# Alternating two kinds of attention steps in a fused two-block transformer kernel

## The chip, the cores and the metric

The kernel runs on one core of a Trainium2 chip. The metric is device time in microseconds (us) for one execution, lower is better. The profile is one execution taken by the hardware profiler; its times count from the first instruction.

## What is computed

Two transformer blocks in float32 on one sequence of 512 positions, width 1024. Only the second mixer of the first block bears on this change:

```python
def odd_mixer(h, ...):
    # eight stick-breaking heads of 64 (o_c), eight latent heads (o_d)
    ...
    q_full = heads(rmsnorm(c_q, q_norm) @ w_uq, H_MLA, NOPE_DIM + ROPE_DIM)
    q_nope, q_rope = q_full[..., :NOPE_DIM], rope(q_full[..., NOPE_DIM:], positions)
    kv_full = heads(rmsnorm(c_kv, kv_norm) @ w_ukv, H_MLA, NOPE_DIM + V_DIM)
    ...
    o = jnp.concatenate([o_c.reshape(b, s, W_SB), o_d.reshape(b, s, W_MLA)], axis=-1)
    return o @ w_out
```

Stick-breaking attention weighs key j for query i with exp(z_ij - sum over k from j to i of softplus(z_ik)). The latent attention is a softmax over chunks of 64, with queries and keys of 96 (64 projected and 32 rotated, the rotated keys shared by all heads).

## The kernel before

Everything is transposed: features in the partitions, the 512 positions in the free dimension. Each weight is streamed once as a slab of 128 x 1024 float32 (8 tiles of 128 x 128). SyncE loads slab m into `raw[m % 2]`; ScalarE copies its two halves to `w_hi` (L1051), rounded; GpSimd subtracts to get `w_lo` (L455). Slab m + 2 is split when the product of slab m is full (`slab_done`, L1053). A product of a tile is three matmuls, high x high, high x low, low x high (L480 to L482; L635 to L637 in `early_out`). Three PSUM banks `gemm_banks` take the projections in a ring that is worked out ahead (`ring`, L115). VectorE evacuates them.

The mixer has 8 pairs of heads, p = 0 to 3 stick-breaking and p = 4 to 7 latent, and four blocks of 128 queries each: 32 steps, `s = 4 p + i`, block i with keys 0 to w = 128 (i + 1). A step's scores for both heads go to two of the four `score_banks` (bank pair b = s % 2). Each engine runs its own program in order; semaphores join them. In iteration s of the loop, TensorE (L811) does: scores of step s (L758, L765), projection tiles (`cd_beside(s, 0)`), transposes of the shares of step s - 1 back into its score banks (`cd_flip`, L773), more tiles, for stick-breaking the mask of step s + 1 as a matmul (`cd_bias`, L746), and the values of step s - 1 into `out_bank` (`cd_values`, L787).

A stick-breaking step: ScalarE computes Abs (L1295), Exp (L1296), Relu (L1302) and Ln (L1303) of the scores of both heads at a time; VectorE scans them from right to left for each head (L1890) and subtracts (L1892); ScalarE takes Exp (L1300). A latent step: VectorE adds the mask and takes row maxima (L1693), ScalarE exponentiates with row sums (L1144), VectorE takes reciprocals (L1904), ScalarE scales (L1152). For both, VectorE copies the turned shares from PSUM (`cd_take`, L1899) before `cd_values` can use them. When the four blocks of a pair are done, ScalarE copies `out_bank` to `u_hi` (L1307) and VectorE subtracts to get `u_lo` (L1908); the next pair's first values wait for that.

`CD_ITEMS` (L182) lists the projections in order: v, q, k of each stick-breaking pair with 8 tiles each, then, for each latent pair, c0, c1 (keys and values of its heads, 2 tiles each) and q0, q1 (3 tiles each), packed without gaps into 5 slabs. Values are transposed on TensorE in between (`vt`). 30 tiles come before step 0; `cd_plan` (L187) gives the rest, by halves of a step: six or seven a step in steps 0 to 10, two or three from step 11 to 26. From step 27 on, `EARLY` (L642) puts tiles of the first two columns of the output projection beside the steps; they need the finished `u_hi`, `u_lo` of a pair.

Of the kernel before, what the change touches and what calls it, by code (L numbers as in the profile page):

```python
# [39 lines left out]
P = 128  # L40
# [134 lines left out]
def half(s, side):  # L175
# [6 lines left out]
CD_ITEMS = [(name, p, 8) for p in range(4) for name in "vqk"] + \  # L182
           [(name, p, n) for p in range(4, 8) for name, n in (("c0", 2), ("c1", 2), ("q0", 3), ("q1", 3))]
STICK_STEPS, CD_STEPS, CD_AHEAD = 16, 32, 30


def cd_plan():  # L187


    at, out = CD_AHEAD, {}  # L190
    for s in range(27):
        if s < 11:
            sides = (4, 2) if s == 0 else ((3, 2), (4, 2), (4, 2), (4, 3))[s % 4]
        else:
            sides = ((1, 2), (1, 1), (1, 1), (1, 2))[(s - 11) % 4]
        for side in range(2):
            out[s, side] = (at, at + sides[side])
            at += sides[side]
    return out
# [9 lines left out]
def cd_evened(s):  # L209

    return 64 + (s + 1 if s < STICK_STEPS else 2 * (s + 1) - STICK_STEPS)
# [74 lines left out]
def build(nc, slabs, x_in, params_in, consts_in, pos1_in, pos2_in, rel_in, lam_in, y_out):  # L286
    n_slabs = slabs.shape[0]
    rel_rows = nc.dram_tensor("rel_rows", (8, E_LEN), F32, kind="Internal").ap()
    with ExitStack() as stack:
# [20 lines left out]
        q_t, k_t = sb("q_t", [2, S], F32, region), sb("k_t", [2, S], F32, region)  # L310
        region.close()
# [6 lines left out]
        V, VT = sb("V", [2, NB, P]), sb("VT", [S])  # L318
# [4 lines left out]
        wf = sb("wf", [KT, 40], F32R)  # L323
# [83 lines left out]
        slab_used = sem("slab_used")  # L407
# [7 lines left out]
        norm_full, mean_ready, gate_ready = sem("norm_full"), sem("mean_ready"), sem("gate_ready")  # L415

# [49 lines left out]
        def _(pe):  # L466
# [156 lines left out]
            def early_out(n, low, high):  # L623
# [4 lines left out]
                for kt in range(low, high):  # L628
                    if kt % 4 == 0:
                        pe.wait_ge(slab_split, c.slab.at(2 * n + 1 + kt // 4, 2))  # L630
                    pe.wait_ge(act_lo, c.lo.at(kt + 1))
# [3 lines left out]
                    pe.matmul(bank, high_w, u_hi[:, kt, :], start=kt == 0, stop=False, skip_group_check=True)  # L635
                    pe.matmul(bank, high_w, u_lo[:, kt, :], start=False, stop=False, skip_group_check=True)
                    last = pe.matmul(bank, low_w, u_hi[:, kt, :], start=False, stop=kt == KT - 1,  # L637
# [67 lines left out]
            marks["cd_lo"] = cd_lo  # L705

            def cd_products(low, high):
                for name, p, j, n in units(CD_ITEMS, low, high):
                    at = cd_banks[name, p]
                    if name == "vt":  # L710
                        pe.wait_ge(gemm_free, done["v" if p < 4 else "c1", p])
                        bank = open_ring(at)
                        for t in range(NB):
                            last = pe.transpose(bank[:, t * P:(t + 1) * P], VT[:, t * P:(t + 1) * P], ident)
                    else:
# [20 lines left out]
                        if j < n - 1:  # L736
                            continue
# [1635 lines left out]
```

## Time and profile before

| | us |
|---|---|
| median of 3 runs (2112.16 to 2114.46) | 2112.99 |
| the profiled execution | 2108.83 |
| its span, first to last instruction | 2107.0 |
| TensorE busy in the span | 2032.5 |
| steps of the mixer that the change touches, from 681 to 880.5 | 199.5 |

TensorE's busy time counts modelled ends of pipelined matmuls, so a start-to-start distance (0.23 us for a 512-column matmul) is shorter than a matmul's shown 0.39 us, and the end of each busy stretch hides a little of the wait behind it. Idle of an engine is put down to what released it last.

### The profile page before, as it was taken

The numbers are of one execution on the slowest core, as the hardware profiler recorded it, in microseconds if no ns is written. First come the engines' busy times: TensorE is split into PE (matmuls) and PEld (weight loads), VectorE is DVE, ScalarE is ACT, GpSimd is POOL, SyncE is SP. The second block draws the span as 40 slices with busy tenths as digits, with TensorE's granted clock in tenths as the row PEclk, the third lists the DMA queues.
The fourth block names the chain that finished last, engine by engine and source line by source line (L and its number), as shares of the span: only waits on it lengthen the run. The fifth ranks groups of instructions, "written<-read, shape, count | busy, mean of one in ns | idle before, by whom it ended". The sixth has DMA issues, their size and how long they took to land.

```text
span 2107.0 us, 28472 instructions
## 1 busy us (share of the span) xinstructions
PE 2032.5 (96%) x9900; PEld 1601.9 (76%) x9900; DVE 972.4 (46%) x1563; ACT 902.2 (43%) x1759; POOL 870.6 (41%) x648
## 2 busy tenths in 40 slices
PE   9999999999999988899999999999999999999997
PEld 6777688888887755688888886766667888888886
DVE  7444545322354678542312265557565653323133
ACT  5444443323344664442323346656554333223234
POOL 3222345444454321254444453542113554445454
PEclk9999999999999999999999999999999999999999
DMA  4222122222222110122322222221111323223323
GB/s 146 71 71 84 57 100 93 97 100 93 97 100 90 61 41 31 41 93 97 100 94 96 100 92 78 90 93 49 40 41 61 100 90 100 100 90 100 100 90 110
DMA packets 50581, 177.88 MB, mean 84 GB/s; under 512 B 5536, under 2 KB 5800, under 8 KB 50480
## 3 DMA queue, kind: packets, MB, share of 16 engines
q1 hardware_dynamic: 48096, 172.07, 24.6%
q10 hardware_dynamic: 2384, 4.43, 0.6%
q8 instruction: 67, 1.10, 0.2%
q14 instruction: 34, 0.28, 0.0%
HBM read 174.36 MB, written 2.12 MB: 84 GB/s over the span
## 4 chain that ended last, share of the span: by engine, by line
issue 47%; PE 30%; POOL 19%; DVE 2%; POOLq 1%; ACT 0%; DVEq 0%; ACTq 0%
POOL w_lo L455 19%; PE gemm_banks L480 9%; PE gemm_banks L481 9%; PE gemm_banks L482 9%; PE score_banks L934 1%; PE out_bank L980 1%; PE score_banks L943 1%; DVE turned L2117 1%; POOLq L449 0%; POOLq L454 0%; PE gemm_banks L906 0%; DVE score_banks L1693 0%; DVE x L2213 0%; PE out_bank L971 0%; ACT tmp L1395 0%
## 5 line engine op out<-in xcount | busy, mean ns | idle before, releaser
L455 POOL TENSOR_TENSOR w_lo<-raw,w_hi 128x512 fp32r<-128x512 f32 x644 | 870.4, 1374 | 1219.2 <-ACT w_hi L1051 1219.1
L1051 ACT ACTIVATE w_hi<-raw 128x512 fp32r<-128x512 f32 x644 | 371.0, 624 | 825.1 <-PE gemm_banks L482 810.0
L480 PE MATMUL gemm_banks<-h_hi,w_hi 128*128 128x512 f32 x1512 | 611.8, 405 | 3.4 <-POOL w_lo L455 3.1
L482 PE MATMUL gemm_banks<-h_hi,w_lo 128*128 128x512 f32 x1512 | 590.5, 391 | 0.0
L481 PE MATMUL gemm_banks<-h_lo,w_hi 128*128 128x512 f32 x1512 | 590.0, 390 | 0.0
L480 PEld LDWEIGHTS gemm_banks<-h_hi,w_hi 128*128 128x128 f32 x1512 | 283.2, 187 | 93.6 <-issue 32.0
L480 PE MATMUL gemm_banks<-u_hi,w_hi 128*128 128x512 f32 x848 | 330.3, 390 | 4.2 <-POOL w_lo L455 2.9
L482 PEld LDWEIGHTS gemm_banks<-h_hi,w_lo 128*128 128x128 f32 x1512 | 282.9, 187 | 62.1
L482 PE MATMUL gemm_banks<-u_hi,w_lo 128*128 128x512 f32 x848 | 329.9, 389 | 0.0
L481 PE MATMUL gemm_banks<-u_lo,w_hi 128*128 128x512 f32 x848 | 329.9, 389 | 0.0
L481 PEld LDWEIGHTS gemm_banks<-h_lo,w_hi 128*128 128x128 f32 x1512 | 283.7, 188 | 56.4 <-issue 2.6
L1601 DVE TENSOR_TENSOR x<-gemm_banks,x 128x512 f32<-128x512 f32 x112 | 77.5, 692 | 308.0 <-PE gemm_banks L482 305.8
L480 PEld LDWEIGHTS gemm_banks<-u_hi,w_hi 128*128 128x128 f32 x848 | 159.1, 188 | 38.9 <-issue 3.7
L482 PEld LDWEIGHTS gemm_banks<-u_hi,w_lo 128*128 128x128 f32 x848 | 159.2, 188 | 33.0
L481 PEld LDWEIGHTS gemm_banks<-u_lo,w_hi 128*128 128x128 f32 x848 | 159.2, 188 | 33.0
L1801 DVE TENSOR_TENSOR u_lo<-tmp,u_hi 128x512 fp32r<-128x512 f32 x86 | 108.6, 1263 | 125.6 <-ACT u_hi L1237 108.7
L1144 ACT ACTIVATE probs<-score_banks,top 128x128 f32<-128x128 f32 (+3 forms) x192 | 99.4, 523 | 140.4 <-DVE top L1693 137.4
L1152 ACT ACTIVATE probs<-probs,share 128x128 f32<-128x128 f32 (+3 forms) x160 | 81.1, 554 | 73.2 <-DVE share L1715 36.1
L1537 DVE TENSOR_TENSOR tmp<-gemm_banks,rstd 128x512 f32<-128x512 f32 x52 | 36.0, 692 | 141.0 <-PE gemm_banks L482 139.6
L1793 DVE SCALAR_TENSOR_TENSOR tmp<-gemm_banks,rstd 128x512 f32<-128x512 f32 x64 | 44.3, 692 | 121.2 <-PE gemm_banks L482 118.5
L1556 DVE TENSOR_TENSOR acc<-acc,sq 128x512 f32<-128x512 f32 x51 | 71.0, 1392 | 10.1 <-ACT sq L1069 9.3
L1693 DVE CUSTOM_DVE_ANT_0 score_banks<-score_banks,sin 128x128 f32<-128x128 f32 (+3 forms) x96 | 45.4, 514 | 35.7 <-PE score_banks L934 35.5
(314 smaller groups left out, 1884.6 us busy)
## 6 DMA issues: line engine op xcount, KB each, us to landing
raw<-slabs SPq DMA_DIRECT2D x322, 512.0 KB, 3.3
table<-rel_rows ACTq DMA_DIRECT2D x4, 512.0 KB, 3.4
x<-x_t SPq DMA_DIRECT2D x4, 256.0 KB, 6.9
x<-x_t ACTq DMA_DIRECT2D x4, 256.0 KB, 7.1
cos<-pos SPq DMA_DIRECT2D x2, 256.0 KB, 10.3
y_t<-x SPq DMA_DIRECT2D x2, 256.0 KB, 2.8
y_t<-x ACTq DMA_DIRECT2D x2, 256.0 KB, 2.7
y_t<-x SPq DMA_DIRECT2D x1, 512.0 KB, 2.8
```

The lines of the kernel that those rows point to most:

```text
L455: pool.tensor_tensor(w_lo[:, j, part], raw[:, j, part], w_hi[:, j, part].bitcast(F32), ALU.subtract).then_inc(slab_split, 1)
L480: pe.matmul(out, high, rhs_hi, start=first, stop=False)
L481: pe.matmul(out, high, rhs_lo, start=False, stop=False)
L482: return pe.matmul(out, low, rhs_hi, start=False, stop=last)
L1051: act.activation(w_hi[:, m % 2, part], raw[:, m % 2, part], ACT.Copy).then_inc(slab_hi, 1)
L1144: act.activation(probs[:, b, head, 0:w], SC[:, 2 * b + head, 0:w], ACT.Exp, bias=top[:, b, head:head + 1], scale=-1.0, accum_out=mass[:, b ...
L1152: act.activation(probs[:, b, head, 0:w], probs[:, b, head, 0:w], ACT.Copy, scale=share[:, b, head:head + 1]).then_inc(evened, 1)
L1556: dve.tensor_tensor(sums[:, :], sums[:, :], sq[:, c.acc.slot, :], ALU.add).then_inc(acc_ready, 1)
L1601: dve.tensor_tensor(x[:, j, :], bank, x[:, j, :], ALU.add).then_inc(gemm_free, 1)
L1693: last = dve.tensor_tensor_reduce(z, z, masks[head], -1.0, 3e38, ALU.add, ALU.min, top[:, b, head:head + 1])
L1793: dve.scalar_tensor_tensor(tmp[:, s, :], result(), 0.0, rstd[:, :], ALU.max, ALU.mult).then_inc(gemm_free, 1)
L1801: dve.tensor_tensor(u_lo[:, j, :], tmp[:, 2 + s, :], u_hi[:, j, :].bitcast(F32), ALU.subtract).then_inc(act_lo, 1)
```

## The change

The 32 steps get a new order: stick-breaking step n, then latent step n - 2. So the order is S0, S1, S2, L0, S3, L1, and so on to S15, L13, L14, L15. Score banks still go by s % 2. The projections are reordered to suit: the latent weights of pair p + 3 are taken before those of stick-breaking pair p. Each latent pair has two slabs of its own (c with 4 tiles, q with 6 tiles), so the stage takes 15 slabs for stick-breaking and latent pairs where it took 12 and 5: three more in all.

- The plan spreads the tiles over steps 0 to 23; the early output tiles, taken in the order in which pairs finish (0, 4, 1, 5, 2, 6, 3, 7), go beside steps 24 to 32.
- The output is handed over by block: after each step ScalarE copies 128 columns of `out_bank` (`cd_mixed(s - 2)`, the first thing in iteration s), VectorE subtracts, and the values of step s wait for that of step s - 1.
- The stick-breaking chain goes by heads: Ln, scan, subtraction and last Exp are issued for one head and then the other, and the transposes of head 0 wait for head 0's shares only. That last Exp is now at the head of the following iteration on ScalarE.
- In a latent iteration that follows a stick-breaking one, VectorE does maxima, output block, take of the stick-breaking shares and reciprocals, and only then evacuates the results of three halves.
- Buffers: stick-breaking q and k in `tmp`, latent values in `V_late`, `VT_late`, `wf` in a region used later; the shared rotated keys are copied in steps 0 and 1.

The core of the diff:

```diff
+for p in range(1, 4):
+    CD_ITEMS += latent("c0", "c1", p=p + 3) + [("v", p, KT)] + latent("q0", "q1", p=p + 3) + [("q", p, KT), ("k", p, KT)]
+CD_ITEMS += latent("c0", "c1", "q0", "q1", p=7)
+CD_ORDER = [(k // NB + 4 * odd, k % NB) for n in range(18) for k, odd in ((n, 0), (n - 2, 1)) if 0 <= k < 16]
+CD_AT = {step: t for t, step in enumerate(CD_ORDER)}
+CD_STEPS, CD_AHEAD = len(CD_ORDER), 31
...
+    twin = ((2, 2), (2, 1), (2, 2), (2, 2), (3, 2), (2, 2), (3, 2), (3, 2))
+    sides = ((4, 2), (4, 2), (2, 2), (2, 2), (3, 2), (2, 2)) + twin + twin + ((2, 2), (2, 2))
...
             def cd_flip(s):
-                pe.wait_ge(evened, cd_evened(s))
                 for head in range(2):
+                    pe.wait_ge(evened, 64 + 2 * s + head + 1)
...
             def cd_values(s):
                 pe.wait_ge(taken, AB_STEPS + s + 1)
                 if i == 0:
                     pe.wait_ge(gemm_free, done["vt", p])
-                    if p >= 1:
-                        pe.wait_ge(act_lo, cd_lo + C_TILES + p)
+                if s >= 1:
+                    pe.wait_ge(block_out, s)
...
+            CD_EARLY = {(24, 0): (0, 0, 1), (24, 1): (0, 1, 2), (25, 0): (0, 2, 3), (25, 1): (0, 3, 4),
+                        (26, 0): (0, 4, 5), (26, 1): (1, 0, 1), (27, 0): (1, 1, 2), (27, 1): (1, 2, 3),
+                        (28, 0): (1, 3, 4), (28, 1): (1, 4, 5), (29, 1): (0, 5, 6), (30, 0): (1, 5, 6),
+                        (31, 1): (0, 6, 7), (32, 0): (1, 6, 7)}
...
+            def stick_shares(s):
+                kind, p, i, b, w = cd_step(s)
+                for head in range(2):
+                    if head == 0:
+                        act.wait_ge(lessened, cd_count("stick", s))
+                    else:
+                        act.wait_ge(maxed, AB_STEPS + s + 1)
+                    act.activation(probs[:, b, head, 0:w], probs[:, b, head, 0:w], ACT.Exp).then_inc(evened, 1)
...
+                for head in range(2):
+                    act.activation(part[:, head, :], part[:, head, :], ACT.Ln, bias=ones[:, 0:1]).then_inc(softened, 1)
...
+            for s in range(CD_STEPS + 2):
+                kind = cd_kind(s)
+                if s >= 2:
+                    cd_mixed(s - 2)
+                if kind == "stick":
+                    soften(s)
+                elif kind == "latent":
+                    if cd_kind(s - 1) == "stick":
+                        stick_shares(s - 1)
+                    weigh(AB_STEPS + s, cd_step(s)[4])
                 cd_products(*cd_half(s, 0))
+                if kind == "latent":
+                    even(s, cd_step(s)[4], AB_STEPS + cd_count("latent", s))
                 cd_products(*cd_half(s, 1))
...
+                    dve.wait_ge(softened, 2 * cd_count("stick", s) + head - 1)
                     back = soft[:, b, head, 0:w][:, ::-1]
+                    link(dve.tensor_tensor_scan(back, back, positive[:, head, 0:w][:, ::-1], 0.0, ALU.add, ALU.add))
+                    last = dve.tensor_tensor(probs[:, b, head, 0:w], z[:, head, :], soft[:, b, head, 0:w], ALU.subtract)
+                    last.then_inc(maxed if head else lessened, 1)
...
+            for s in range(CD_STEPS + 2):
+                kind = cd_kind(s)
+                twin = kind == "latent" and cd_kind(s - 1) == "stick"
+                if kind == "latent":
+                    w = cd_step(s)[4]
+                    maxima(AB_STEPS + s, w, [chunk_mask[:, S - w:S]] * 2)
+                if s >= 2:
+                    cd_mixed(s - 2)
+                if twin:
+                    cd_take(s - 1)
+                    cd_shares(s)
+                    cd_evacuated(*cd_half(s - 1, 1))
+                cd_evacuated(*cd_half(s, 0))
+                if not twin and 1 <= s <= CD_STEPS:
+                    cd_take(s - 1)
+                if kind == "stick":
+                    stick(s)
+                elif kind == "latent" and not twin:
+                    cd_shares(s)
+                if cd_kind(s) != "stick" or cd_kind(s + 1) != "latent":
+                    cd_evacuated(*cd_half(s, 1))
```

## Rows read from the trace of the kernel before

**Rows 1.** The page, part 1: busy us of the engines, share of the span.

```profile
PE 2032.5 (96%) x9900; PEld 1601.9 (76%) x9900; DVE 972.4 (46%) x1563; ACT 902.2 (43%) x1759; POOL 870.6 (41%) x648
```

**Rows 2.** Busy us by window: length, PE, PEld, DVE, ACT, POOL, PEclk, DMA share, GB/s.

```profile
681.00:755.80 74.80, 73.67 (x422) 54.09 (x420) 48.35 (x56) 47.32 (x74) 23.11 (x17) 1.00 0.19 64
755.80:850.00 94.20, 75.20 (x451) 52.07 (x449) 76.97 (x146) 49.23 (x105) 12.56 (x10) 0.96 0.09 29
850.00:880.50 30.50, 26.05 (x167) 17.91 (x165) 15.16 (x37) 13.73 (x35) 2.96 (x2) 1.00 0.06 18
...
780.00:790.00 10.00, 7.78 (x43) 5.42 (x43) 9.63 (x11) 5.72 (x7) 3.44 (x2) 0.83 0.15 52
```

**Rows 3.** Waits from 681 to 882 us: who waited for whom, total us, times, longest.

```profile
POOL w_lo L455 <- ACT w_hi L1051: 161.7, 15, 27.5
...
PE out_bank L787 <- DVE turned L1899: 11.8, 14, 2.4
PE score_banks L773 <- ACT probs L1300: 10.7, 7, 2.2
```

**Rows 4.** Timeline of PE, a dense stretch: start us, us, engine, line, operation.

```profile
726.12 0.66 PE L787 MATMUL out_bank<-turned,V 128*64 128x128 f32 x8
726.71 1.13 PE L765 MATMUL score_banks<-k_t,q_t 64*128 64x512 f32 x4
727.77 0.50 PE L480 MATMUL gemm_banks<-h_hi,w_hi 128*128 128x512 f32 x1
...
728.57 0.40 PE L480 MATMUL gemm_banks<-h_hi,w_hi 128*128 128x512 f32 x1
...
729.26 0.39 PE L480 MATMUL gemm_banks<-h_hi,w_hi 128*128 128x512 f32 x1
```

**Rows 5.** Timeline of PE, a thin stretch (idle before and releaser in brackets).

```profile
785.77 1.54 PE L773 MATMUL score_banks<-consts,probs 128*128 128x128 f32 x6 [2.22 <-ACT probs L1300]
786.96 0.78 PE L480 MATMUL gemm_banks<-cn_hi,w_hi 128*128 128x512 f32 x1
...
793.13 1.09 PE L773 MATMUL score_banks<-consts,probs 128*128 128x128 f32 x8 [1.41 <-ACT probs L1300]
793.98 0.48 PE L480 MATMUL gemm_banks<-cn_hi,w_hi 128*128 128x512 f32 x1
```

**Rows 6.** Groups of VectorE by form, 680 to 882 us: busy us, mean ns.

```profile
L1899 DVE COPY turned<-score_banks 128x1024 f32<-128x1024 f32 x8 | 9.8, 1225 | 8.6 <-PE score_banks L773 5.0 <-issue 3.6
L1890 DVE TENSOR_TENSOR_SCAN soft<-soft,c_raw 128x512 f32<-128x512 f32 x8 | 9.4, 1212 | 0.1
...
L1876 DVE SCALAR_TENSOR_TENSOR tmp<-gemm_banks,sin 32x512 f32<-32x512 f32 x8 | 5.6, 695 | 0.1
...
L1693 DVE CUSTOM_DVE_ANT_0 score_banks<-score_banks,c_raw 128x512 f32<-128x512 f32 x8 | 5.5, 702 | 2.0 <-PE score_banks L758 1.9
L1899 DVE COPY turned<-score_banks 128x512 f32<-128x512 f32 x8 | 5.5, 690 | 5.7 <-PE score_banks L773 5.7
...
L1899 DVE COPY turned<-score_banks 128x256 f32<-128x256 f32 x8 | 3.3, 417 | 1.6 <-PE score_banks L773 1.5
```

**Rows 7.** Groups of ScalarE by form, the same stretch.

```profile
L1303 ACT ACTIVATE soft<-soft,consts 128x1024 f32<-128x1024 f32 x4 | 4.6, 1142 | 0.0
...
L1296 ACT ACTIVATE soft<-soft 128x1024 f32<-128x1024 f32 x4 | 4.2, 1060 | 0.1
...
L1295 ACT ACTIVATE soft<-score_banks 128x1024 f32<-128x1024 f32 x4 | 4.1, 1028 | 4.0 <-PE score_banks L765 4.0
L1302 ACT ACTIVATE c_raw<-score_banks 128x1024 f32<-128x1024 f32 x4 | 4.0, 1005 | 0.0
```

**Rows 8.** Timelines of GpSimd (POOL) and VectorE: two 128-column scans, twice.

```profile
710.92 2.64 POOL L455 TENSOR_TENSOR w_lo<-raw,w_hi 128x512 fp32r<-128x512 f32 x2 [9.31 <-ACT w_hi L1051]
...
712.04 1.80 DVE L1890 TENSOR_TENSOR_SCAN soft<-soft,c_raw 128x128 f32<-128x128 f32 x2
...
769.18 0.73 DVE L1890 TENSOR_TENSOR_SCAN soft<-soft,c_raw 128x128 f32<-128x128 f32 x2
```

More of the change, by code:

```diff
@@ L206, in cd_half, with cd_step, cd_kind, cd_count @@
     return CD_PLAN.get((s, side), (0, 0))
-def cd_evened(s):
-    return 64 + (s + 1 if s < STICK_STEPS else 2 * (s + 1) - STICK_STEPS)
+def cd_step(s):
+    p, i = CD_ORDER[s]
+    return "stick" if p < 4 else "latent", p, i, s % 2, (i + 1) * P
+def cd_kind(s):
+    return cd_step(s)[0] if 0 <= s < CD_STEPS else None
+def cd_count(kind, s):
+    return sum(cd_kind(n) == kind for n in range(s + 1))
 E_BASE, DIFF_STEPS, E_STEPS, E_AHEAD = 64, 16, 48, 6
@@ L627, in early_out @@
                     pe.wait_ge(gemm_free, c.gemm.at(n - 1))
[L628 to L631, printed above, removed]
+                for k in range(low, high):
+                    kt = k
+                    if mixed is not None:
+                        kt = mixed[k]
+                        if k == 0:
+                            pe.wait_ge(slab_split, c.slab.at(2 * n + 2, 2))
+                        pe.wait_ge(block_out, CD_AT[kt, NB - 1] + 1)
+                    else:
+                        if kt % 4 == 0:
+                            pe.wait_ge(slab_split, c.slab.at(2 * n + 1 + kt // 4, 2))
+                        pe.wait_ge(act_lo, c.lo.at(kt + 1))
                     w_slot = (c.slab.now + n) % 2
@@ L817, in _ @@
                 cd_beside(s, 1)
-                if s + 1 < STICK_STEPS:
+                if cd_kind(s + 1) == "stick":
                     cd_bias(s + 1)
@@ L1854, in cd_evacuated @@
                     c.gemm.now += 1
-                    if p >= 4 and name != "vt":
-                        dve.wait_ge(scored, 64 + 8 * (p - 1))
                     if name == "vt":
-                        if p >= 2:
-                            dve.wait_ge(valued, 64 + 8 * (p - 1))
-                        last = dve.tensor_copy(V[:, p % 2, :, :], bank)
+                        if p not in (0, 1, 4, 5):
+                            dve.wait_ge(valued, 64 + 2 * (CD_AT[p - 2, NB - 1] + 1))
+                        last = dve.tensor_copy(cd_values_of(p), bank)
                     elif name == "v":
@@ L2261, in pack_slabs @@
     out += column_tiles(cq) + [slab(np.concatenate([kr, kr[:, 16:], kr[:, :16]], 1))] + column_tiles(ckv)
-    out += heads(w, 0)
-    tiles = []
-    for p in range(4):
-        pair = []
-        for h in (2 * p, 2 * p + 1):
-            uq, ukv = a["w_uq"][0][:, 96 * h:96 * h + 96], a["w_ukv"][0][:, P * h:P * (h + 1)]
-            pair.append((tiles_of(ukv), tiles_of(np.concatenate([uq, uq[:, 80:96], uq[:, 64:80]], 1))))
-        tiles += [t for part in range(2) for head in pair for t in head[part].transpose(1, 0, 2)]
-    out += [np.ascontiguousarray(np.stack(tiles[k:k + 8], 1)).reshape(P, SLAB) for k in range(0, len(tiles), 8)]
+    plain = heads(w, 0)
+    late = {}
+    for p in range(4, 8):
+        for part, wide in enumerate((P, 96)):
+            pair = []
+            for h in (2 * p - 8, 2 * p - 7):
+                if part == 0:
+                    m = a["w_ukv"][0][:, P * h:P * (h + 1)]
+                else:
+                    m = a["w_uq"][0][:, wide * h:wide * (h + 1)]
+                    m = np.concatenate([m, m[:, 80:96], m[:, 64:80]], 1)
+                pair.append(m)
+            late["cq"[part], p] = slab(np.concatenate(pair, 0))
+    for name, p, n in CD_ITEMS:
+        if p < 4:
+            out.append(plain[3 * p + "vqk".index(name)])
+        elif name in ("c0", "q0"):
+            out.append(late[name[0], p])
     out += column_tiles(a["w_out_cd"][0]) + mlp(1)
```

209 lines of the change are left out of this document (77 added, 132 removed).

## The prediction

> **What bounds the kernel now.** The page first: TensorE (PE) has work for 96% of the span [rows 1], so time can only come from its gaps, and from work that moves into them. The windows of the stage that is changed show where they are [rows 2]. The stage runs from 681 to 880.5 us, 199.5 us. Its first 11 steps (681 to 755.8) are dense: PE idles 1.1 of 74.8 us. From 755.8 to 850 it idles 19.0 of 94.2 us, from 850 to 880.5 another 4.4 of 30.5. The waits name two causes, on PE [rows 3]: `cd_values` waits for the copy of the turned shares (VectorE, 11.8 us), `cd_flip` for the last Exp of a stick-breaking step (10.7 us). In the first 11 steps the same chain is hidden by projection tiles: a tile of three matmuls costs 0.69 us from start to start (728.57 to 729.26), 0.80 where it is the first after other work (727.77 to 728.57) [rows 4], and there are 66 of them beside 11 steps, six a step. From step 11 on two or three stand beside a step, while the latent steps come one after another. So the bound is latency for want of filler, not any engine's capacity: VectorE, the next busiest, is busy 48.4 + 77.0 + 15.2 = 140.5 of 199.5 us [rows 2]. The idle also lowers PE's clock: six turns after a wait of 2.22 us take 1.19 us (785.77 to 786.96), where eight took 0.85 at 793.13, and the granted clock from 780 to 790 is 0.83 of 2.4 GHz, that is, part of it at 1.2 GHz [rows 2, 5].
>
> **PE's own demand.** 66 tiles x 0.69 = 45.5 us of the first 74.8; less 1.1 idle, the other 28.2 us are eleven steps' scores, turns, values and first-tile surcharges, some 2.5 us a step. Before, the stage holds 106 projection tiles and 16 early output tiles: 122 x 0.69 = 84, and 32 x 2.5 = 80, together 164. The stage therefore loses 199.5 - 164 = 35.5 us: 24.6 seen as idle, the rest hidden under modelled matmul ends and in the slower clock. That is all that the change can win.
>
> **1. The order.** Each latent step now follows a stick-breaking step two ahead of it, so the tiles are spread evenly: 105 beside steps 0 to 23 (4.4 a step), then output tiles, two a step in steps 24 to 28 and one a step in 29 to 32. Demand is 105 x 0.69 + 24 x 2.5 = 132.5 us for steps 0 to 23, 11.0 us a pair of steps, and 31 us for the tail. No instruction of PE is added or removed but one tile that moves ahead of the stage, where PE is busy: no gain from it.
>
> VectorE is what must keep pace. To its 140.5 us come: outputs by blocks of 128 columns, 32 subtractions where 8 were; a PSUM pass takes 0.690 for 512 columns and 0.417 for 256 [rows 6], so 0.28 for 128: 32 x 0.28 - 8 x 0.69 = +3.5. The stick-breaking subtraction by heads costs one fixed part more, 2 x 0.417 - 0.690 = 0.14, x 16 = +2.3. Some 2 us of waits between scan and subtraction make it 148. The tail has no evacuations; at the durations of [rows 6] it holds nine takes (7.4), three steps' scans and subtractions (8.7), five steps' maxima (6.0) and small work (3): 25 us. That leaves 123 us for steps 0 to 23, 10.2 us a pair against PE's 11.0. Engines in order at 93% of each other do meet. Two places are visible in the plan: the turned values vt5 and vt6 (steps 9, 17) open a bank whose evacuation (v2, v3) is queued on VectorE behind the stick-breaking take and `cd_shares`, 1 to 2 us each; and around steps 9 to 10 and 17 to 18 two latent q results of 4 x 0.695 = 2.8 us each [rows 6] stand ahead of a take.
>
> What a pair loses is not in the trace. Bounds: nothing (the dense stretch loses 0.1 a step), or all in series, in the rival below. The rows between which it lies: 0.1 us a step at six tiles, 19.0/16 = 1.2 a step at 2.5 tiles; at 4.4 tiles that is 0.6 a step, 1.2 a pair. The chain is also shorter (2.), so I take 1.0: 12 us for twelve pairs.
>
> **2. The chain by heads.** Before, a 512-wide stick-breaking step needs from its scores to its turns Abs 1.03, Exp 1.06, Relu 1.00, Ln 1.14 [rows 7], with the step before's Exp among them, two scans of 1.21, a subtraction of 1.22 and an Exp of 1.06: 8.9 us and more. By heads the first head is ready after 1.03 + 1.06 + 1.00 + 0.57 + 1.21 + 0.69 + 0.53 = 6.1 us, the second after another scan and subtraction, 8.0 us. PE does the rest of step s and the first half of step s + 1 between these scores and their turns, 1.3 steps of 5.5, some 7 us in the middle of the stage: head 0 is covered and head 1 nearly. That the Exp is now behind the copy of the last output block costs nothing: that block's values end before the next scores, two PE items ahead of the turns.
>
> **3. The tail.** Steps 24 to 27 have two tiles each: I take 0.5 lost a step, 2 us. Step 28 is the last stick-breaking one, 512 wide, and PE has only two tiles, 1.6, small turns and values, 0.6, and the next scores, 0.8, before it needs the shares: 3.0 us. It waits about 8.0 - 3.0 - 0.4 = 4.6 us. The latent steps 29 to 32 have one tile where [rows 2] had two beside them and idled 4.4 us in six steps: 0.73 + 0.69 = 1.4 each, 5.7 us. The tail loses 12.3 in all.
>
> **4. Three more weight slabs** (latent weights no longer share slabs: 5 become 8), each with a 512 KB load, two ScalarE copies and two GpSimd subtractions. GpSimd waits 161.7 us for ScalarE in this stage [rows 3], and a slab of four latent tiles lasts PE about a step, 5 us, against the 2.6 us in which GpSimd splits one [rows 8]: taken at nothing; the upper bound is GpSimd's six operations in the open, 3 x 2.6 = 7.9 us, which stays inside the range. There is a side cost. Two scans of 128 columns take 0.73 us by themselves and 1.80 when they start beside the subtraction of w_lo [rows 8]. The Trainium skill, "SBUF — State Buffer" (Who interferes with whom), says that a VectorE instruction with two SBUF inputs blocks against a GpSimd one that reads SBUF; by it six more subtractions would give up to six more such blockings, an estimate of one subtraction's length each, and it speaks against the change. In the rows the delay is 1.80 - 0.73 = 1.07 us for a pair of scans, so at most 3.2 us of VectorE's time for three slabs. Scans (0.73 to 2.4 us a step, 16 steps) take 25 us, 13% of the stage, so most slabs meet none; what is left is inside the 1.0 a pair.
>
> **The sum.** Steps 0 to 23: 132.5 + 12 = 144.5; tail: 31 + 12.3 = 43.3; the stage 187.8 us against 199.5: 11.7 us less. The profiled execution took 2108.83 us with a span of 2107.0; it becomes 2097.1. The median of the runs is 4.2 us above it, and I put the same difference on that: 2113.0 - 11.7 = **2101.3 us**.
>
> **Rivals.** A: the pairs mesh, losing 0.2 a pair or less; only the tail costs. 132.5 + 2 + 43.3 = 178: 2091.5, or 2089 if half of step 28's wait is covered by head 0. For it: the first stretch loses next to nothing; against it: VectorE at 93%. B, little changes: a pair costs 12.7 to 13.4 us, because the late evacuations and blocked scans of 1. and 4. come in every pair and not in four. 2109 to 2117, about 2112. Against it: evacuations are 42 us (in steps 0 to 23 16 single ones, 6 results c of two operations and 8 results q of four, 60 x 0.695), a third of VectorE's work. C, slower: VectorE's queue puts everything into one loop in every pair: the take waits for the turns, with evacuations, maxima and the next stick-breaking step behind it. For 512 columns the loop is 8.0 + turns 0.85 + take 1.23 + values 1.2 (eight take 0.59) + scores 1.06 = 12.3 [rows 4 to 7]; over the four widths about 0.7 of it, 8.6; evacuations 42/12 = 3.5; maxima and output block 1.5: 13.6 a pair. 12 x 13.6 + 43.3 = 206.5, so 2120.0. It decides from 13.4 a pair on ((199.5 + 4.2 - 43.3)/12). Against it: maxima run while ScalarE and PE do the Exp and turns, and most evacuations while ScalarE softens.
>
> **Chances.** A measurement of this kernel can tell 0.2%, 4.2 us, from no change. The forecast, a pair between 11.2 and 12.7 us: 0.60; A 0.17; B 0.13; C 0.10. So faster 0.77, same 0.13, slower 0.10. Range 2089 to 2112: from A with a better tail to the middle of B.
>
> **What would show it.** Right: PE's waits in the stage fall from 24 to about 15 us; most sit after step 24, the longest, over 3 us, before the last stick-breaking turns; VectorE is busy about nine tenths of steps 0 to 23; the half clock shows only in the tail. The rest of the kernel keeps its length. Wrong: waits of over 1 us in each pair at `cd_flip` (chain) or at opening a bank (late evacuations), or PE waiting on w_lo in the stage (slabs).

## The result, and the profile after

The changed kernel took 2115.6 us (median of 20 runs), the kernel before 2112.9 (20 runs of its own): ratio 1.0015, 95% interval 1.0009 to 1.0022. The forecast was 2101.3 us and faster. The kernel became slower by about 3 us. That is less than the 4.2 us that the prediction needs to tell a time from no change, and it lies above the top of its range, 2112 us.

The profiled execution has a span of 2113.8 us, 6.8 more than before. 2.6 us of that is no part of the change: up to the norm matmul that opens this part of the mixer both kernels run the same instructions, and it stands at 670.12 us before, 672.75 after, and between 669.6 and 673.6 in the kernels below. All lengths here are therefore counted from that matmul to the first slab of the output projection that waits for its split weights ("norm to slab"): 670.12 to 882.15 = 212.0 us before, 672.75 to 888.58 = 215.8 after, 3.8 more. Of these, 2.6 lie ahead of the first mask matmul (10.89 us before, 13.46 after) and 1.2 in the steps. Behind the slab the two kernels are equal within 0.4 us.

The page, part 1, of the changed kernel (before: [rows 1]):

```profile
PE 2038.5 (96%) x9900; PEld 1604.6 (76%) x9900; DVE 974.3 (46%) x1603; ACT 914.3 (43%) x1821; POOL 877.6 (42%) x654
```

Windows of the changed kernel, columns as in [rows 2]: ahead of the steps, steps 0 to 23, a period of eight steps, the tail, and two stretches of the tail.

```profile
670.00:686.20 16.20, 14.94 (x64) 11.32 (x63) 14.06 (x20) 7.78 (x13) 6.29 (x5) 1.00 0.28 98
686.20:831.90 145.70, 134.69 (x792) 97.61 (x790) 109.91 (x209) 92.95 (x210) 42.16 (x32) 1.00 0.18 58
723.50:771.80 48.30, 45.07 (x271) 32.69 (x270) 36.05 (x71) 31.25 (x71) 13.72 (x11) 1.00 0.17 55
831.90:887.00 55.10, 40.85 (x242) 26.64 (x240) 31.09 (x65) 28.24 (x65) 2.94 (x2) 0.91 0.03 10
834.00:845.00 11.00, 8.29 (x38) 5.31 (x38) 8.77 (x18) 3.28 (x10) 1.33 (x1) 0.84 0.15 48
860.00:875.00 15.00, 9.98 (x52) 6.82 (x50) 7.84 (x17) 7.18 (x18) 0.00 (x0) 0.77 0.00 0
```

Steps 0 to 23 took 145.7 us where 144.5 was forecast: twelve pairs at 12.1, as the period of four pairs shows (48.3). The tail took 55.0 us (831.92 to 886.95) where 43.3 was forecast. And VectorE is busy 109.9 of 145.7 us, 75%, not nine tenths.

Waits of the changed kernel, 670 to 889 us (before: [rows 3]):

```profile
POOL w_lo L489 <- ACT w_hi L1088: 165.9, 20, 51.8
...
PE out_bank L823 <- DVE turned L1927: 9.1, 11, 1.7
...
PE score_banks L808 <- ACT probs L1317: 9.0, 9, 3.3
...
PE gemm_banks L754 <- DVE VT L1891: 2.7, 2, 1.3
...
PE gemm_banks L676 <- DVE c_raw L1889: 2.4, 1, 2.4
```

The two large groups fell by 2.7 and 1.7 us, and two new ones came: openings of a projection bank. The sum did not fall. PE's waits from the timeline are 11.0 us in steps 0 to 23 and 14.2 in the tail. Timeline of PE, one wait of steps 0 to 23 and those that open the tail and step 28's turns:

```profile
745.17 0.63 PE L754 MATMUL gemm_banks<-consts,c_raw 128*128 128x128 f32 x4 [1.33 <-DVE VT L1891]
...
831.92 0.70 PE L800 MATMUL score_banks<-tmp 64*128 64x256 f32 x4
834.98 0.50 PE L676 MATMUL gemm_banks<-u_hi,w_hi 128*128 128x512 f32 x1 [2.36 <-DVE c_raw L1889]
...
839.02 0.88 PE L823 MATMUL out_bank<-turned,V_late 128*64 128x128 f32 x12 [1.73 <-DVE turned L1927]
...
843.00 0.63 PE L677 MATMUL gemm_banks<-u_lo,w_hi 128*128 128x512 f32 x1
...
849.31 0.40 PE L678 MATMUL gemm_banks<-u_hi,w_lo 128*128 128x512 f32 x1
850.33 1.09 PE L823 MATMUL out_bank<-turned,V_late 128*64 128x128 f32 x16 [0.62 <-DVE turned L1927]
...
864.45 1.02 PE L808 MATMUL score_banks<-consts,probs 128*128 128x128 f32 x4 [3.31 <-ACT probs L1317]
866.31 1.12 PE L808 MATMUL score_banks<-consts,probs 128*128 128x128 f32 x4 [0.83 <-ACT probs L1317]
```

VectorE over the first two waits of the tail:

```profile
830.67 0.69 DVE L1902 SCALAR_TENSOR_TENSOR QT<-gemm_banks,cos 32x512 f32<-32x512 f32 x1
...
832.80 1.40 DVE L1907 TENSOR_TENSOR QT<-QT,kr 32x512 f32<-32x512 f32 x1
834.24 0.69 DVE L1889 COPY c_raw<-gemm_banks 128x512 f32<-128x512 f32 x1
834.96 0.69 DVE L1902 SCALAR_TENSOR_TENSOR QM<-gemm_banks,cos 32x512 f32<-32x512 f32 x1
...
837.09 0.68 DVE L1907 TENSOR_TENSOR QM<-QM,kr 32x512 f32<-32x512 f32 x1
837.81 0.29 DVE L1937 TENSOR_TENSOR u_lo<-out_bank,u_hi 128x128 fp32r<-128x128 f32 x1
838.02 0.95 DVE L1927 COPY turned<-score_banks 128x768 f32<-128x768 f32 x1
```

From 830.67 to 837.8 VectorE works off the last three results of the projections, 9 operations, though no step needs the two queries before step 27. The take of step 23's turned shares stands behind them; its turns ended at 836.4. PE waits for a bank, then for the take, and then runs at the half clock (843.00 to 843.42 between two matmuls, where they take 0.23 at 2.4 GHz). Windows of 2 us show two such stretches in the tail, from 841 to 844 and from 865 to 871, and none in steps 0 to 23.

### The profile page after: what moved, and what is told of

Its sections match the earlier page's. It is cut to its first block, busy times and chain, and to the rows that moved or that the text cites. A ratio compares the mean times of both kernels' runs of the same rounds, so it can differ in the third digit from the quotient of the medians.

```text
span 2113.8 us, 28584 instructions
## 1 busy us (share of the span) xinstructions
PE 2038.5 (96%) x9900; PEld 1604.6 (76%) x9900; DVE 974.3 (46%) x1603; ACT 914.3 (43%) x1821; POOL 877.6 (42%) x654
## 4 chain that ended last, share of the span: by engine, by line
issue 46%; PE 31%; POOL 19%; DVE 2%; POOLq 1%; ACT 0%; DVEq 0%; ACTq 0%
POOL w_lo L489 19%; PE gemm_banks L514 9%; PE gemm_banks L516 9%; PE gemm_banks L515 9%; PE score_banks L971 1%; PE out_bank L1017 1%; PE score_banks L980 1%; DVE turned L2146 1%; POOLq L483 0%; POOLq L488 0%; PE gemm_banks L943 0%; DVE score_banks L1723 0%; DVE x L2242 0%; PE out_bank L1008 0%; ACT tmp L1425 0%
```

## The experiments

The theory after this reading: the steps are as forecast, and the tail loses to (a) evacuations ahead of the take and (b) two tiles a step where step 28 leaves PE 3.3 us with nothing. Its rival: VectorE's load bounds the pairs, and the tail only shows it. Each kernel is timed against the kernel before; "norm to slab" is of its one profiled execution, in which 2 us can be the clock alone (last section).

| kernel | median, us | ratio (95%) | norm to slab |
|---|---|---|---|
| before | 2111.0 to 2112.9 | 1 | 212.0 |
| changed | 2115.6 | 1.0015 (1.0009 to 1.0022) | 215.8 |
| e1_tail | 2109.5 | 0.9992 (0.9983 to 1.0000) | 211.8 |
| e2_pre | 2115.3 | 1.0016 (1.0006 to 1.0025) | 216.2 |
| e3_joint | 2122.7 | 1.0057 (1.0043 to 1.0070) | 223.5 |
| e4_heads | 2110.3 | 0.9999 (0.9990 to 1.0008) | 212.2 |
| e5_less | 2106.5 | 0.9976 (0.9967 to 0.9985) | 208.4 |
| e6_take_first | 2113.6 | 1.0008 (0.9999 to 1.0017) | 216.1 |
| e7_swap | 2117.6 | 1.0029 (1.0017 to 1.0041) | 221.6 |
| e8_bank | 2114.9 | 1.0013 (1.0003 to 1.0024) | 215.9 |
| e9_last | 2108.8 | 0.9986 (0.9977 to 0.9995) | 211.7 |
| e10_value | 2107.2 | 0.9979 (0.9969 to 0.9989) | 208.3 |
| e11_less7 | 2110.0 | 0.9990 (0.9981 to 1.0000) | 212.3 |

**e1_tail**: the last projections over four steps, output tiles later.

```diff
-    sides = ((4, 2), (4, 2), (2, 2), (2, 2), (3, 2), (2, 2)) + twin + twin + ((2, 2), (2, 2))
+    sides = ((4, 2), (4, 2), (2, 2), (2, 2), (3, 2), (2, 2)) + twin + twin + ((1, 1), (1, 1), (1, 1), (1, 1))
...
+            CD_EARLY = {(26, 0): (0, 0, 1), (26, 1): (0, 1, 2), (27, 0): (0, 2, 3), (27, 1): (0, 3, 4),
+                        (28, 0): (0, 4, 6), (28, 1): (1, 0, 2), (29, 0): (1, 2, 4), (29, 1): (1, 4, 5),
+                        (30, 0): (1, 5, 6), (31, 1): (0, 6, 7), (32, 0): (1, 6, 7)}
```

> The changed kernel with other filler at the end: the last eight projection tiles go one to a half over steps 22 to 25, and the output tiles start at step 26, with six of them between the scores of step 28 and its turns. Theory T (the tail): in the changed kernel steps 0 to 23 take what was forecast (145.7 us), and the gain is lost after step 24, where the last evacuations stand in front of a take (PE waits of 2.36 and 1.73 us), where the last stick-breaking step waits 4.1 us, and where PE twice runs at half clock. Then this kernel is about 7 us faster than the changed one: 2108 to 2109, ratio 0.998 to kernel before; the wait before the turns of step 28 falls from 4.1 to about 1.5 us and the one of 2.36 us goes. Rival V (VectorE's time as such is the bound): the waits move to other steps, the ratio stays at 1.0015.

4.1 us less than the changed kernel in norm to slab, and 0.0023 less in the ratio, some 5 us, where 7 were expected. Its PE timeline: the first wait did not go but moved on to the take, and step 28's fell from 3.31 + 0.83 to 0.55 + 1.20. In all, PE's waits in the tail fell from 14.2 to 11.0 us, and the time at the half clock from 10 to 7.

```profile
832.98 0.88 PE L823 MATMUL out_bank<-turned,V_late 128*64 128x128 f32 x12 [2.84 <-DVE turned L1926]
...
859.55 0.66 PE L808 MATMUL score_banks<-consts,probs 128*128 128x128 f32 x4 [0.55 <-ACT probs L1316]
861.40 0.70 PE L808 MATMUL score_banks<-consts,probs 128*128 128x128 f32 x4 [1.20 <-ACT probs L1316]
```

**e2_pre**: v of pair 1 goes ahead of the first latent c tiles, so that these, and their waits, leave the stretch ahead of step 0.

```diff
-    CD_ITEMS += latent("c0", "c1", p=p + 3) + [("v", p, KT)] + latent("q0", "q1", p=p + 3) + [("q", p, KT), ("k", p, KT)]
+    CD_ITEMS += ([("v", p, KT)] if p == 1 else []) + latent("c0", "c1", p=p + 3) + ([("v", p, KT)] if p > 1 else [])
+    CD_ITEMS += latent("q0", "q1", p=p + 3) + [("q", p, KT), ("k", p, KT)]
```

> The changed kernel with the v result of stick-breaking pair 1 ahead of the first latent c results, so that no latent tile stands before step 0. Theory P: in the changed kernel the distance from the second norm matmul to the first mask matmul grew from 10.9 to 13.5 us, 0.7 for the tile moved and 1.3 of waits (0.38 and 0.88 us) at latent tiles whose inputs or bank are late; here it is 12.1 to 12.3 and the kernel 1.3 us faster than the changed one, ratio 1.0009. Rival: VectorE has the same work in steps 0 and 1 and the wait comes back there (beyond the 0.77 us at the first stick-breaking q tile): ratio 1.0015.

The norm to first mask fell from 13.46 to 11.58 us, and the steps grew from 202.4 to 204.6. The ratio stayed, 1.0016, as the rival said. Up to step 4 its PE timeline has, among others, waits of 0.24 and 0.47 us, which are new, and of 1.27 and 1.73 us, which were 0.77 and 1.28; and from 708 to 711 us PE ran at the half clock:

```profile
689.32 0.48 PE L515 MATMUL gemm_banks<-cn_hi,w_hi 128*128 128x512 f32 x1 [0.24 <-POOL w_lo L490]
693.82 0.63 PE L755 MATMUL gemm_banks<-consts,c_raw 128*128 128x128 f32 x4 [0.47 <-DVE c_raw L1900]
```

The work of the latent c results has to pass VectorE before step 3 either way; where it stands settles which matmul waits.

**e3_joint**: the changed kernel with Ln, scans, subtraction, Exp and turns for both heads together, as before. **e4_heads**: the kernel before with its chain by heads, nothing else.

```diff
-                    pe.wait_ge(evened, 64 + 2 * s + head + 1)
+                pe.wait_ge(evened, 64 + 2 * s + 2)
...
-                    last = dve.tensor_tensor(probs[:, b, head, 0:w], z[:, head, :], soft[:, b, head, 0:w], ALU.subtract)
+                dve.tensor_tensor(probs[:, b, :, 0:w], z, soft[:, b, :, 0:w], ALU.subtract).then_inc(maxed, 1)
```

> The changed kernel with one part undone: Ln, subtraction and last Exp of a stick-breaking step for both heads at a time, turns wait for both. Theory H (the split chain is worth its cost): a 512-wide step's shares are ready about 1.5 us later, and the steps of 384 and 512 columns (8 of 16) wait 0.7 to 1.5 us more at their turns: 6 us slower than the changed kernel, ratio 1.004. Rival F (the fixed parts of the extra instructions, 2.3 us on VectorE and as much on ScalarE, eat it): ratio 1.001 to 1.002.

> The kernel before with one part of the change alone: Ln, subtraction and last Exp of a stick-breaking step by heads, the turns of head 0 wait for head 0's shares only; order, plan and outputs as before. Theory H: of the 10.7 us that PE waits there for the last Exp, steps 11 to 15 give back about 1 us each: 5 us faster than before, ratio 0.9976. Rival F: more instructions on busy engines, nothing gained: 1.000.

PE's waits of e3_joint, and of e4_heads:

```profile
PE score_banks L808 <- ACT probs L1313: 18.1, 9, 5.9
PE out_bank L823 <- DVE turned L1922: 7.8, 11, 1.4
```

```profile
PE out_bank L787 <- DVE turned L1906: 11.7, 12, 3.3
PE score_banks L773 <- ACT probs L1304: 6.8, 6, 1.9
PE score_banks L746 <- DVE turned L1906: 2.3, 3, 1.7
```

The window of e4_heads to set beside the second of [rows 2]:

```profile
755.00:850.00 95.00, 78.54 (x446) 54.32 (x444) 76.25 (x149) 49.49 (x114) 13.99 (x10) 0.91 0.08 28
```

By heads is worth 7.6 us in the new order (223.5 against 215.8; 6.1 of them by step 24) and nothing in the old one. There the waits for shares fell from 10.7 [rows 3] to 6.8 us, single waits for the take rose to 3.3, and all of PE's waits in the stage fell by 3.1 us, from 23.9 to 20.8. The stage did not become shorter because PE ran at the half clock more: the granted clock was 0.91 in that window and 0.96 before, which is 8.6 against 3.8 us of full-speed time missing. The other executions bear it out: over all eleven of e4_heads the mean granted clock is 0.990, and over those of the kernel before beside them 0.992. That is again between 4 and 5 us of full-speed time. Why the clock fell although PE waited less is open.

**e5_less** leaves out the sine part of the latent queries' rotation and its addition (L1904, L1907) for all pairs; **e11_less7** leaves them out for the last pair alone.

```diff
-                        dve.scalar_tensor_tensor(kr[64:96, :], bank[96:128, :], MLA_SCALE, sin1[96:128, :], ALU.mult,
-                                                 ALU.mult)
-                        link(dve.tensor_scalar(dst[0:64, :], bank[0:64, :], MLA_SCALE, None, ALU.mult))
-                        last = dve.tensor_tensor(dst[64:96, :], dst[64:96, :], kr[64:96, :], ALU.add)
+                        last = dve.tensor_scalar(dst[0:64, :], bank[0:64, :], MLA_SCALE, None, ALU.mult)
```

> This kernel leaves out the sine part of the latent queries' rotation and the addition behind it: two of the four VectorE operations on each latent query result, some 16 x 0.69 = 11 us of VectorE's time in steps 0 to 23, and nothing of TensorE's. Theory (in steps 0 to 23 TensorE's own demand and the single waits at bank openings bound, the tail loses by what stands ahead of the take): steps 0 to 23 fall by 0 to 3 us only (a period of eight steps 47.5 to 48.3 us against 48.31), the tail by under 1.5 us; time 2111.5 to 2114.5 us. Rival (VectorE, nine tenths busy, bounds the pairs): its 11 us come back, steps 0 to 23 about 136 us, time about 2105 us.

> The changed kernel, which leaves out the sine part of the rotation and its addition for the last pair's two query results alone: four VectorE operations, 2.8 us, the last of them in iterations 23 and 24. Theory (the tail's first 8 us lose by evacuations that stand ahead of the take of step 23): step 24 to step 26 falls from 14.40 to about 9.6 us, as where this was left out in all pairs, more than the 2.8 us of the operations, since TensorE's half-speed stretch goes with the wait; all else is unchanged; 4.8 us less, about 2110.8 us, ratio 0.999 to 1.0. Rival (VectorE's load over the whole stage gave the gain): 0.25 of the 8 us, 2113.5 us, ratio 1.0005 to 1.0012.

e5_less is 0.0039, some 8 us, below the changed kernel in the ratio and 7.4 us in norm to slab, far more than the theory had expected and nearly what the rival had. But its timeline says where: 2.8 us ahead of step 4 (its scores at 36.51 us behind the norm matmul, not 39.29), 4.8 us between the scores of steps 24 and 26 (9.56, not 14.40), and nothing in a period: 48.31 us, as in the changed kernel, with four operations, 2.8 us, less for VectorE in it. So ahead of step 4 VectorE's load does count, 2.8 us for 2.8: there it is busy 33.1 of the 39.3 us from the norm matmul on, and PE's waits up to step 4 are 2.95 us. e11_less7 leaves that place alone: 9.56 us from step 24 to 26, and all before it as in the changed kernel. Its PE timeline:

```profile
829.67 0.50 PE L676 MATMUL gemm_banks<-u_hi,w_hi 128*128 128x512 f32 x1 [0.19 <-DVE c_raw L1889]
...
832.34 0.88 PE L823 MATMUL out_bank<-turned,V_late 128*64 128x128 f32 x12 [0.36 <-DVE turned L1930]
```

2.36 and 1.73 became 0.19 and 0.36 us, 3.5 less, and the half clock behind them went too. So four operations of 2.8 us (3.5 with the long one) cost 4.8. At the slab 3.5 of the 4.8 are left: half of the rest went where PE ran at the half clock once more, from 878 us on. The rival, a load over the whole stage, is out: a load that bounds could not be cut in the middle without effect. The theory of e5_less was wrong in a size: it gave the tail under 1.5 us.

**e8_bank**: the changed kernel, where the first output tile of the tail takes its bank without waiting for the last value tile's evacuation.

```diff
-                    pe.wait_ge(gemm_free, c.gemm.at(n - 1))
+                    pe.wait_ge(gemm_free, c.gemm.at(n - 1 if mixed is None or n else -2))
```

> The changed kernel, where the first output tile of the tail takes its bank without waiting for the last value tile's evacuation (2.36 us). Theory: what stands behind is late anyway, since the take of step 23 stands behind three evacuations: the wait moves on to the values, stage length unchanged within 0.7 us, 2115 to 2115.6 us. Rival (the opened bank alone costs the 2.36 us): 2113.2 us, ratio 1.0003.

```profile
833.26 0.50 PE L676 MATMUL gemm_banks<-u_hi,w_hi 128*128 128x512 f32 x1 [1.63 <-DVE QT L1907]
838.02 0.88 PE L823 MATMUL out_bank<-turned,V_late 128*64 128x128 f32 x12 [2.46 <-DVE turned L1927]
```

2.36 + 1.73 became 1.63 + 2.46: the same 4.09 us. To open the bank 0.7 us earlier gains nothing; the take's place in VectorE's queue sets the time.

**e6_take_first** (on e1_tail) and **e7_swap** (on the changed kernel): VectorE takes ahead of the projection half in every iteration without a latent step behind a stick-breaking one.

```diff
-                cd_evacuated(*cd_half(s, 0))
                 if not twin and 1 <= s <= CD_STEPS:
                     cd_take(s - 1)
+                cd_evacuated(*cd_half(s, 0))
```

> The tail's filler as in the run with the spread sides, and in every iteration that has no latent step behind a stick-breaking one VectorE takes the turned shares before it evacuates the projection half. Theory (the take waits in VectorE's queue behind evacuations that nothing needs yet): the wait of 2.84 us ahead of values(23) and the waits of 0.5 us in the middle go, 3 us less than with the spread sides alone: about 2106.5 us, ratio to the kernel before 0.9975 to 0.9985, norm matmul to end of stage 208.5 to 209.5 us against 211.77. Rival (the flips' end sets the take, and its order in the queue changes nothing, or the evacuation that is now later holds the next bank and the wait moves there): 2109.5 us, as with the spread sides.

> The changed kernel with the order of VectorE's take and projection half alone swapped in the iterations without a latent step behind a stick-breaking one. Theory: the 0.5 us waits in the middle go (some three to five of them), the tail's 2.36 and 1.73 us stay, since these evacuations belong to an iteration with a latent step: 1 to 2 us less than the changed kernel, 2113.5 to 2114.5 us, ratio 1.0007 to 1.0012. Rival (order of no account): 2115.5 us, ratio 1.0015.

Both were slower than what they started from, by 4.3 and 5.8 us in norm to slab (0.0016 and 0.0014 in the ratio, 3.4 and 3.0 us; the profiled execution of e7_swap is 2.8 us above its median). By step 24 it was 4.4 and 5.4: neither theory had that. VectorE, and then PE, of e6_take_first:

```profile
748.64 0.29 DVE L1936 TENSOR_TENSOR u_lo<-out_bank,u_hi 128x128 fp32r<-128x128 f32 x1
751.32 1.23 DVE L1926 COPY turned<-score_banks 128x1024 f32<-128x1024 f32 x1 [2.39 <-PE score_banks L808]
752.57 0.69 DVE L1901 SCALAR_TENSOR_TENSOR QM<-gemm_banks,cos 32x512 f32<-32x512 f32 x1
```

```profile
698.18 0.50 PE L514 MATMUL gemm_banks<-h_hi,w_hi 128*128 128x512 f32 x1 [2.65 <-DVE QT L1906]
...
755.48 0.46 PE L793 MATMUL score_banks<-KT,QT 96*128 96x128 f32 x2 [1.79 <-issue]
```

A take that stands first waits for the turns, 2.39 us in which VectorE could have evacuated; the next latent scores need that query and come 1.8 us late. The expectation had counted the 0.5 us waits that would go and not what would then wait. The waits are the smaller part, though: in steps 0 to 23 they sum to 12.4 us against 10.7 in e1_tail, and to 11.3 against 11.0 in e7_swap. The larger part goes with the half clock, which came behind some of the long waits (from 700 and 806 us in e6_take_first; from 699, 757 and 808 in e7_swap) and which neither e1_tail nor the changed kernel has before the tail: the granted clock of steps 0 to 23 is 0.98 and 0.95 against 1.00. Only where the query is not needed soon is the swap a gain: from step 24 to 26 e6 took 11.8 us, e1_tail 13.6. The next two use this.

**e9_last**: e1_tail, and the take first in iteration 24 alone. **e10_value**: e9_last, and in iterations 9 and 17 the value tile is evacuated ahead of the reciprocals.

```diff
-                    cd_shares(s)
-                    cd_evacuated(*cd_half(s - 1, 1))
+                    if s in (9, 17):
+                        cd_evacuated(*cd_half(s - 1, 1))
+                        cd_shares(s)
+                    else:
+                        cd_shares(s)
+                        cd_evacuated(*cd_half(s - 1, 1))
+                if s == 24:
+                    cd_take(s - 1)
                 cd_evacuated(*cd_half(s, 0))
-                if not twin and 1 <= s <= CD_STEPS:
+                if not twin and 1 <= s <= CD_STEPS and s != 24:
```

> The kernel with the spread sides, where VectorE takes the turned shares ahead of the projection half in iteration 24 alone (there the half is the last rotated query, four operations). Theory (each such swap is worth what the tile's evacuation held up, less what then waits for the evacuation; in iteration 24 nothing needs that query before iteration 27): step 24 to step 26 takes 11.8 us as with the swap everywhere, against 13.57, and the stage's other parts stay as with the spread sides: norm matmul to the end of the stage 206.5 to 208 us (third tile behind the last values) against 209.44; time about 2107.7 us, ratio 0.998 to 0.9988. Rival: the swap brings nothing in sum, since the scores behind are late by as much: 2109.5 us, ratio 0.9992.

> As the run before, and in iterations 9 and 17 VectorE evacuates the value tile, for whose bank TensorE waits 1.33 us, ahead of the reciprocals, which there wait 0.40 us for ScalarE. Theory: each of the two waits falls by some 0.5 us, since the evacuation starts at the end of the take instead of behind wait and reciprocal; the eight-step period falls from 48.3 to 47.8 us, the time by 1 us to some 2106.7, ratio 0.9975 to 0.9985. Rival: the reciprocals come 0.3 to 0.5 us later, with them the scaled shares and their turns, and the period stays 48.3 us; 2107.7 us.

In e9_last step 24 to 26 fell to 11.9 us as expected, but norm to slab by 0.1 only: its tail has three stretches at the half clock (from 838, 862 and 879 us), that of e1_tail has two, and from step 28's scores to the slab it took 32.4 us against 31.0. e10_value, VectorE and PE in iteration 9:

```profile
740.05 0.69 DVE L1926 COPY turned<-score_banks 128x512 f32<-128x512 f32 x1 [0.29 <-PE score_banks L808]
740.65 0.68 DVE L1890 TENSOR_TENSOR VT<-gemm_banks,rstd 128x512 f32<-128x512 f32 x1
741.37 0.17 DVE L1931 RECIPROCAL share<-mass 128x2 f32<-128x2 f32 x1
```

```profile
741.48 0.63 PE L754 MATMUL gemm_banks<-consts,c_raw 128*128 128x128 f32 x4 [0.78 <-DVE VT L1890]
```

1.33 became 0.78 us, twice, and steps 0 to 23 fell by 1.2 us, a period from 48.3 to 47.7. The other 2.3 us that norm to slab is below e9_last are clock (last section). This version beats both kernels, if by 0.2% only: its interval of ratios, 0.9969 to 0.9989, lies below 1 and below that of the changed kernel. Against e9_last the intervals overlap. Its windows, steps 0 to 23 and tail:

```profile
683.04:824.50 141.46, 131.79 (x776) 94.84 (x774) 106.15 (x204) 91.62 (x207) 42.10 (x32) 1.00 0.17 57
824.50:876.40 51.90, 40.43 (x258) 26.54 (x256) 33.33 (x69) 29.73 (x68) 2.96 (x2) 1.00 0.06 20
```

## Why the prediction was wrong

From the norm matmul to the slab the forecast was 11.7 us less, and the profiled executions show 3.8 more. The 15.5 us between them are 2.6 ahead of step 0, 1.2 in steps 0 to 23 and 11.7 in the tail.

**Steps 0 to 23 were right**: 145.7 against 144.5 us, 11.0 us of visible waits against 12 lost. Most places were right too: openings for the turned values in iterations 9 and 17, 1.33 us each (forecast 1 to 2), and shares or takes late around 10 and 18 by 0.5 us. The reason given for them was half wrong: VectorE was to be nine tenths busy and is 75%. Its total of 141.0 us in steps and tail is that of before (140.5 [rows 2]) and not 148: blocks and heads did add, but the first c results (2.8 us) moved ahead of step 0, the scans took 2.4 us less, and 2 us of the 148 were waits. And the tail holds 31 us, not 25. From step 4 on, what costs is the order at a few places, not the load, as the unchanged period of e5_less shows. Not foreseen were the waits up to step 4, 2.95 us, where the same run shows VectorE's load to count.

**The term that failed is the tail**, "tail: 31 + 12.3 = 43.3" (31 of demand, 12.3 of loss), with 55.0 measured. Term by term:
- "I take 0.5 lost a step, 2 us" for steps 24 to 27: 6.0 us of waits (2.36, 1.73, 0.62, 0.91, 0.35). The prediction said "the tail has no evacuations". But the tiles of the last half of step 23 are evacuated in the tail, and two of the last three results are queries with four operations each. e11_less7 shows it: 4.8 us. The same queue had been priced for steps 9 and 17 and was forgotten here.
- The half clock was foreseen in the tail and priced at nothing. A granted clock of 0.84 over 11 us and of 0.77 over 15 us means 3.5 and 6.9 us at 1.2 GHz. Half of such time is lost, less what PE waits in it: some 4 us, an estimate. The first stretch's part of it is inside e11_less7's 4.8.
- Step 28: 4.6 us forecast, 3.31 + 0.83 = 4.1 measured. Steps 29 to 32: 5.7 forecast, 0.83 + 1.16 + 1.32 + 0.73 = 4.0 measured. Both right within their size.
- The demand, "31 us for the tail": 55.0 less 14.2 of waits and some 4 of clock leaves 37. e10_value, whose tail runs at 2.4 GHz throughout, agrees: 51.9 us from step 24's scores to the end of the steps, less 11.5 of waits and four more tiles (2.8), is 37.6. Not all of it is demand. A stop costs more than its shown wait: from 849.31 to 850.33 pass 1.02 us, of which a matmul takes 0.23 and the wait is given as 0.62, so 0.17 is hidden. Over the tail this sums to some 2.6 us, an estimate from the start-to-start distances of the same items where no wait follows. That leaves some 34.5, 3.5 more than forecast. Reasons visible in the rows, not tested: the turns and values of step 23 (0.58 and 0.81 us) fall into the tail, and the 2.5 us a step come from eleven stick-breaking steps of some 300 columns, while the tail's steps are 368 columns wide on average and five of the eight are latent. A latent step's scores of 512 columns take 1.83 us, in the rows below, and a stick-breaking one's 1.06 [rows 4].

```profile
875.13 1.12 PE L793 MATMUL score_banks<-KT,QT 96*128 96x512 f32 x2
876.10 1.02 PE L793 MATMUL score_banks<-KM,QM 96*128 96x512 f32 x2
876.96 0.82 PE L808 MATMUL score_banks<-consts,probs 128*128 128x128 f32 x6
```

Together: 4 (steps 24 to 27) + 4 (clock) - 2 (steps 28 to 32) + 2.6 (hidden) + 3.5 (demand) = 12 us, the 11.7 that are missing. The first term is shown by an experiment. The clock is read from the rows; the last two are estimates and, with the clock, not separated by one.

**"No gain from it", one tile that moves ahead**, was held at nothing and cost 2.6 us: the tile's 0.69, 0.38 of issue and 0.88 of waiting for VectorE, and the rest around these two stops. VectorE is busy 11.4 of the 13.5 us from the norm matmul to the first mask (8.7 of 10.9 before). e2_pre shows that it cannot be had back simply by moving the tiles.

**By heads** had no price of its own but stood behind the 1.0 a pair; e3_joint shows that this rests on it: a period of eight steps takes 50.4 us without it, 48.3 with it. **Three more slabs at nothing** was right: GpSimd still waits 165.9 us for ScalarE, PE's only wait for `w_lo` is the one behind the stage, 1.47 us as before, and the scans take 31.5 us in all against 33.9 before (the prediction had counted 25 for them). Ten of the 32 scans still met a slab's subtraction and took 0.3 to 0.7 us longer than their like, 5.4 us in all against 9.2 before. So did the rotated query's addition at 832.80, 1.40 us against 0.68 for the same at 837.09: 0.7 us in the worst place. GpSimd beside it:

```profile
832.39 2.94 POOL L489 TENSOR_TENSOR w_lo<-raw,w_hi 128x512 fp32r<-128x512 f32 x2 [5.20 <-ACT w_hi L1088]
```

The Trainium skill's page "SBUF — State Buffer" (Who interferes with whom) lists exactly this pair, a VectorE instruction with two SBUF inputs against a GpSimd one that reads SBUF, as contending; this row agrees.

The check named in the prediction, "PE's waits in the stage fall from 24 to about 15", failed: they sum to 25.2. So did "VectorE is busy about nine tenths". Held did that most waits sit after step 24, the longest, 3.31 us, before the last stick-breaking turns, and that the half clock shows only in the tail. That the rest of the kernel keeps its length held behind the stage (0.4 us) but not ahead of step 0 (2.6 us). Of the rivals none happened. The time lies in the 2109 to 2117 of B, but by chance: a pair costs 12.1 us, not the 12.7 to 13.4 that B needs.

So the gain was not hidden: the change does what it says in 24 steps, and gives it back in the eight that follow, where the filler is used up, plus 2.6 us ahead of the first. With the filler spread and VectorE's queue reordered in three iterations, the same change is 4 to 5 us faster than the kernel before. Some 3.5 of the forecast 11.7 us were never there, by the estimate above, since the demand of the tail was put too low.

## What to carry to other kernels

When filler is spread evenly over a loop, price the drain by its own instruction list, result by result, and not by the averages of the full stretch: the last results are evacuated after their tiles, in front of what the next step needs. Moving a copy forward in an in-order queue is a gain only where what falls behind it has slack; check for each place who needs that and when, and change only the places with slack. An engine at 75% can hold up the others at a few points: here, cutting its load in the eight-step periods gave nothing, and the same cut ahead of step 4 and in the drain gave 2.8 and 4.8 us. Compare the granted clock before a difference is put down to waits: in e4_heads, e6_take_first and e7_swap it moved by more than the waits did.

## What the runs showed of the hardware

The clock that TensorE is granted differs between executions of one kernel. Of the 20 of the changed kernel the two slowest (2118.7 and 2119.8 us) have the lowest mean clock, 0.987 and 0.986, and the four fastest (2112.2 to 2113.3 us) have 0.991 to 0.993.

Nor does it follow from the instructions and waits at hand alone. In e9_last and e10_value the tail from step 28 on is the same program with the same waits to 0.1 us, up to the slab's (0.88 and 1.47 us). e9_last had one stretch at the half clock before, from 838 to 841, and e10_value none. Windows of seven us around the same values and scores, e9_last and then e10_value (granted clock is the third column from the end):

```profile
860.00:867.00 7.00, 6.38 (x34) 4.52 (x34) 2.33 (x7) 2.20 (x7) 0.00 (x0) 0.76 0.00 0
```

```profile
857.00:864.00 7.00, 5.29 (x38) 3.68 (x40) 3.65 (x11) 3.40 (x11) 0.00 (x0) 1.00 0.00 0
```

After waits of 0.56, 1.20 and 0.61 us the one runs partly at 1.2 GHz and the other at 2.4; a second such stretch follows at 879. From step 28's scores to the slab the one takes 32.4 us and the other 30.1. So 2.3 us between two profiled executions can be clock alone, as much as what was tried in e9_last. That is why its gain of 1.7 us does not show in norm to slab. The Trainium skill's page "TensorE: Matmul & The Clock Gate" (Part 1: The HAM clock gate) says of a kernel's start that the number of slow matmuls of one kernel varies from run to run. The 20 executions agree in kind; the two windows, of two kernels and in mid-kernel, show the like at another place.
